# TensorE multiplies the identity into free banks, a fixed number of times, at nineteen places where it waits in norms, routers and at the end of the experts

## What is computed

```python
def layer_norm(x, g, b):
    mu = xf.mean(-1, keepdims=True)
    var = jnp.square(xf - mu).mean(-1, keepdims=True)
    y = (xf - mu) * lax.rsqrt(var + LN_EPS) * g + b
def moe(h, router_w, router_b, w_gate, w_up, w_down):
    aff = jax.nn.sigmoid((x @ router_w))
    sel_score = aff + router_b
    ...  # the best of 4 groups of experts, in it the best 2 of 4: chosen
    w = aff * chosen / sum
    for e in range(N_EXPERTS):                       # 16 experts, width 512
        he = (silu(x @ w_gate[e]) * (x @ w_up[e])) @ w_down[e]
        y = y + w[:, e:e + 1] * he
def first_block(...):
    for l in range(DEPTH):                           # 2 layers
        mix = retention(h, ...) if l < 1 else nsa_attention(h, ...)
        h = layer_norm(ALPHA * h + mix, ln_mix_g[l], ln_mix_b[l])
        h = layer_norm(ALPHA * h + moe(h, ...), ln_ffn_g[l], ln_ffn_b[l])
def second_block(...):
    mix = (gates[0] * y_ssd + gates[1] * y_att) @ w_out
    h = layer_norm_2(alpha * h + mix, ln1_g, ln1_b)
    f = jnp.square(relu(h @ w_up)) @ w_down
    h = layer_norm_2(alpha * h + f, ln2_g, ln2_b)
```

## Time and profile before

| | |
|---|---|
| median of 3 runs | 1574.66 us (1574.34 to 1576.18) |
| the profiled execution: its time | 1574.03 us |
| its span, first to last instruction | 1572.2 us |
| PE busy | 1426.0 us, 91% |
| DVE busy | 774.6 us, 49% |
| ACT busy | 557.0 us, 35% |
| mean granted clock of PE | 0.945 |

### The profile page before, as it was taken

How to read it: one execution, slowest core, us unless ns; L and a number is a source line. 1 busy time by engine, 2 the same in 40 slices (tenths; PEclk the granted TensorE clock), 3 DMA queues, 4 the chain that set the end, 5 groups by cost and what they waited for, 6 DMA issues and landing times. The chain is left out here.

```text
span 1572.2 us, 19843 instructions
## 1 busy us (share of the span) xinstructions
PE 1426.0 (91%) x8494; PEld 1066.1 (68%) x8494; DVE 774.6 (49%) x1040; ACT 557.0 (35%) x778; POOL 63.5 (4%) x73
## 2 busy tenths in 40 slices
PE   6999978999968989969999959999888899799996
PEld 6986764344326778854444339898867799699985
DVE  4646551222235647541221253599668865655545
ACT  3344321111012444321101023588447753335432
POOL 0000010000002000010000020000022100000000
PEclk9999978999997989969999969999898999999998
DMA  8544775999982520459999964423212135435451
GB/s 330 211 163 161 276 285 207 429 426 429 428 381 100 209 113 1 161 241 398 427 428 428 427 282 148 174 108 126 101 43 108 54 116 207 161 135 190 186 198 43
DMA packets 27600, 355.23 MB, mean 226 GB/s; under 512 B 2864, under 2 KB 4912, under 8 KB 5616
## 3 DMA queue, kind: packets, MB, share of 16 engines
q1 hardware_dynamic: 25696, 341.85, 54.4%
q0 software_dynamic: 1808, 12.01, 1.9%
HBM read 352.80 MB, written 1.05 MB: 225 GB/s over the span
## 5 line engine op out<-in xcount | busy, mean ns | idle before, releaser
L1931 DVE TENSOR_TENSOR ring_low<-ring,w_rounded 128x2048 fp32r<-128x2048 f32 (+1 forms) x128 | 291.3, 2276 | 318.6 <-ACT w_rounded L1479 310.7
L1479 ACT ACTIVATE w_rounded<-ring 128x2048 fp32r<-128x2048 f32 (+1 forms) x128 | 243.0, 1900 | 358.6 <-PE ps L826 128.3
L826 PE MATMUL ps<-split,w_rounded 128*128 128x256 f32 x1056 | 254.7, 291 | 22.7 <-DVE ring_low L1931 17.1
L826 PE MATMUL ps<-split,ring_low 128*128 128x256 f32 x800 | 231.4, 289 | 0.0
L826 PEld LDWEIGHTS ps<-split,w_rounded 128*128 128x128 f32 x1056 | 189.5, 197 | 25.1 <-issue 19.6
L842 PE MATMUL ps<-w_rounded,split 128*128 128x512 f32 (+1 forms) x448 | 157.0, 400 | 8.0 <-DVE ring_low L1931 3.4
L826 PE MATMUL ps<-hT_low,w_rounded 128*128 128x256 f32 x544 | 157.5, 289 | 0.0
L826 PEld LDWEIGHTS ps<-split,ring_low 128*128 128x128 f32 x800 | 157.4, 197 | 0.0
L842 PE MATMUL ps<-ring_low,split 128*128 128x512 f32 (+1 forms) x304 | 119.1, 392 | 0.0
L2171 DVE TENSOR_SCALAR split<-ps,work 128x1024 fp32r<-128x1024 f32 x14 | 18.0, 1284 | 197.6 <-PE ps L1014 197.6
L826 PEld LDWEIGHTS ps<-hT_low,w_rounded 128*128 128x128 f32 x544 | 108.3, 199 | 0.0
(11 more groups left out here) (333 smaller groups left out, 2206.9 us busy)
## 6 DMA issues: line engine op xcount, KB each, us to landing
ring<-slabs SPq DMA_DIRECT2D x65, 2048.0 KB, 7.8
work<-experts_w SPq DMA_DIRECT2D x48, 2048.0 KB, 20.3
ring<-experts_w SPq DMA_DIRECT2D x36, 2048.0 KB, 16.9
w_plain<-experts_w SPq DMA_DIRECT2D x12, 2048.0 KB, 16.7
gb<-ln_gb POOLq DMA_DIRECT2D x6, 1024.0 KB, 7.9
ring<-slabs SPq DMA_DIRECT2D x2, 1024.0 KB, 8.8
hT<-x_feat SPq DMA_DIRECT2D x1, 1024.0 KB, 5.1
work<-c_ret POOLq DMA_DIRECT2D x1, 1024.0 KB, 11.9
```

The costliest lines, as they stand in the source:

```text
L826: last = nc.tensor.matmul(dst[:, at:at + T], w3[a][:, k, c * P:(c + 1) * P], src[b][:, k, :], start=(k == 0 and t == 0), stop=(k == KC - 1 ...
L1479: nc.scalar.activation(rounded_half(q), half_of(ring, q), ACT.Copy).then_inc(w_high, 1)
L1931: V.tensor_tensor(half_of(ring_low, q), half_of(ring, q), rounded_half(q).bitcast(F32), ALU.subtract).then_inc(w_low, 1)
```

## The change

A helper `idle_products(dst, n)` issues n plain f32 products of the identity with the identity repeated twice (256 moving columns) into a PSUM bank which nothing reads before it is written anew. No semaphore is signalled by them. They stand ahead of waits: before each tile's transposes in norms 0 to 4 and after the last of them (table `IDLE`), before the position products (8), before the first gather (3), and before `scatter_tail` (13). That is 14 + 21 + 10 + 21 + 20 = 86 in the norms and 2 x (8 + 3 + 13) = 48 in the rest, 134 in all. Where n is 0 behind the transposes nothing is issued, but `take_aux` still adds its wait for the first transposed bank to be free, which `wait_transposed` waits for as well.

```diff
+            def idle_products(dst, n):
+
+                out2 = dst[:, 0:2 * P].rearrange("p (a n) -> p a n", a=2)
+                for _ in range(n):
+                    nc.tensor.matmul(out2, ident, ident.unsqueeze(1).broadcast_to([P, 2, P]), start=True, stop=True)
+
+            IDLE = {"ln0": (9, 5, 0), "ln1": (12, 5, 4), "ln2": (5, 5, 0), "ln3": (12, 5, 4), "ln4": (10, 4, 6)}
+
             def tokens_to_features(stage, src, groups, ready, first):
 
                 for i in range(NT):
+                    after_experts = i == 0 and stage in ("ln1", "ln3")
+                    idle_products(bank(0) if after_experts else take_aux(AX[stage] + groups * i), IDLE[stage][i])
                     pe.wait_ge(ready, first + i)
                     for c in range(groups):
                         transpose4(AX[stage] + groups * i + c,
...
             def norm_to_features(n):
                 tokens_to_features(f"ln{n}", h, 2, h_ready, 2 * n + 1)
+                idle_products(take_aux(AX[f"ln{n}"] + 4), IDLE[f"ln{n}"][2])
                 wait_transposed(f"ln{n}", 4)
...
                 if q is None:
+                    idle_products(bank(0), 13)
                     scatter_tail(e2)
...
                 pos = take_aux(AX[f"router{layer}"] + 1)
+                idle_products(pos, 8)
                 pe.wait_ge(member_ready, layer + 1)
...
                 pe.wait_ge(token_low, NT * layer + NT)
+                idle_products(bank(0), 3)
                 expert_pass(passes[layer][0])
```

## The result

The changed kernel's median is **1563.18 us** (1559.5 to 1566.05, 5 runs) against 1574.88 (1574.34 to 1576.18, 5 runs) before: ratio 0.9919, 95% interval 0.9899 to 0.9939. It is 11.7 us faster, where 17.7 were forecast. The profiled execution took 1561.76 us, 12.27 less than that of before.

The account below looks back on a forecast made before the run. The clock halved at norms and routers, so PE waited and then worked slowly. Products in the waits would give back 6.6 + 6.4 + 4.5 + 4.5 + 1.7 = 23.7 us, less 6.0 for routers: 17.7, to 1557 us, range 1550 to 1567.

Parts of the forecast that it names:

- Price of a product, 0.43: On PE, a product of two records takes 0.43 us at full clock, 0.86 at 1.2 GHz.
- What hides the products: At the norms, routers and experts' ends, each group at 0.43 us a product fits PE's wait; at 0.86 none fits.
- Norm 4, 1.7: After norm 4, 17 records of `up` would run at full clock, gaining 1.7 us; its second transposes nothing.
- Second transposes, 0.88: In four norms, the second eight transposes would take 1.09 us instead of 1.97, gaining 0.88 each.
- Routers, 6.6 and 6.4 less 3.0 each: Norms with routers 0 and 1 gain 6.6 and 6.4 us, less 3.0 each as the clock falls within the router.
- the row: At 228 to 230 PE was busy all 2.00 us with 16-column router records, yet the clock stayed at 0.50.
- Does the gain reach the end?: The gain was to reach the end: the experts' slab stream moves with PE, and later projections are PE's own chain.
- the case forecast: Whole kernel: products hold the clock but it falls within the routers; 1553 to 1563 us, chance 0.60.
- rival (c): Routers cost about what they give, the clock falling before them; 5 to 11 us gained, 1563 to 1569, chance 0.17.
- (d): Slower: products don't hold the clock, each takes 0.86 and overruns its wait; about 48 us, 1622, chance 0.06.
- (e): No change: the clock falls as before between groups, which stay hidden in their waits; chance 0.04.
- Rival (b): The clock holds through the routers too; the full 23.7 us gained, 1551 us, chance 0.13.

Follow-up runs that it names:

- e2: The changed kernel with as many products at the same places, each moving 16 columns instead of 256; 1576.59 us, ratio 1.0009 to before.
- e8: The changed kernel with 20 products instead of 9 ahead of norm 0's first transposes; 1564.17 us in a single execution.
- e1: The changed kernel with the twelve products of norms 1 and 3 ahead of the overflow branch instead of behind it; 1558.62 us, ratio 0.9901 to before.
- e6: e5 plus two products between the second transposes and the router in norms 0 and 2; 1550.70 us, ratio 0.9857 to before.
- e5: e1 with norm 4's last six products sent to bank 0, which is free all that time; 1560.47 us, ratio 0.9906 to before.
- e11: The changed kernel plus only the two products behind the second transposes of norms 0 and 2; 1559.35 us, ratio 0.9898 to before.
- e10: The kernel of e6 measured again, unchanged; 1549.78 us, ratio 0.9837 to before.
- e9: The kernel of e5 measured again, unchanged; 1560.08 us, ratio 0.9906 to before.
- e12: e6 with six products instead of eight ahead of the positions; 1557.13 us, ratio 0.9876 to before.
- e7: e5 with five products instead of eight ahead of the positions; 1554.49 us, ratio 0.9878 to before.
- e3: The changed kernel with only the 8 + 3 products of each router left; 1574.19 us, ratio 0.9988 to before.
- e4: The changed kernel with only the products of the norms left, none of the 13, 8 and 3; 1570.12 us, ratio 0.9967 to before.

## Why the prediction came out as it did

**What bounds the kernel, and that the gain is the clock.** Right. e2 has as many products with fewer columns, a clock that fell ahead of the router all the same, and no gain.

**Price of a product, 0.43.** Right: 0.216 a record in after, and e8.

**What hides the products.** Right for norms 0, 2 and the 13; wrong for the twelve at the end of the experts. The step that failed is "end of the experts, ... 12 in 5.2 of 5.98": it took the wait of the earlier trace rows as free for PE from its first microsecond. 3.3 to 4.8 us at the start of it were the branch, and nothing that stands behind it was issued meanwhile. The products started 2.98 and 4.12 us late, at a clock that had fallen, and the places gave 2.75 and 1.20 us instead of 4.5 each. That is 5.0 of the missing time. With the products ahead of the branch norm 1 gives 4.52 (e1), and norm 3 gives 4.41 in e6, where the stall that cut it to 2.85 in e1 is absent: the term itself was right.

**Norm 4, 1.7.** Sized right, but the text on the kernel held that `take_aux` adds only a wait that is there anyway. For products ahead of `wait_transposed` it is a new one, 1.71 us, and it made `up` 0.4 us late: 1.07. With a free bank 1.57 (e5).

**Second transposes, 0.88.** Right (1.97 to 1.09 in norm 0). They gained at a clock held by the products, and so against the sentence of the Trainium skill (TensorE: Matmul & The Clock Gate, Part 4) that the full clock doesn't engage for transposes.

**Routers, 6.6 and 6.4 less 3.0 each.** The full terms are right almost to the tenth: 32.12 - 25.50 = 6.62 in e11 and 29.80 - 23.16 = 6.64 in e6. The fall inside the router is right too. The loss was smaller than 3.0 in the profile of after: 2.5 and 0.6, because the router fell late (0.6 and 0.1 lost, not 1.6) and the gather did not suffer at all. One part was too low, positions 1.92 late in router 0 instead of 0.9: the rise took longer than the 3.3 us taken from the gather (the eight began at 231.92, and 235 to 238 still shows 0.59). The small loss is in part the luck of one execution: e5 and e11 lost 2.5 in router 1 as well (25.64 and 25.66). In after the clock fell within the router while PE was busy with it, and in e2 it stayed at 0.50 over 10.4 us of narrow products back to back. Both speak for the row, and against the rule of the Trainium skill (TensorE: Matmul & The Clock Gate, Part 1), time in sustained matmul activity, as the prediction applied it.

**Does the gain reach the end?** Right within the experts: 0.04 and 0.27 us were lost in some 217 each. But the last 65 us of sparse attention, untouched, took 3.06 us more. The stretch 640 to 650, in before and in after:

```profile
640.00:650.00 10.00, 10.00 (x66) 8.79 (x66) 5.86 (x16) 1.09 (x2) 0.00 (x0) 1.00 0.27 115
```

```profile
640.00:650.00 10.00, 10.00 (x34) 8.07 (x34) 1.83 (x6) 0.00 (x0) 0.00 (x0) 0.66 0.50 182
```

In after the clock is down for a part of it. Those 65 us last 65.1, 66.7 or 68.2 us in each of the fourteen profiles, and both ends occur with kernels that differ by nothing ahead of it (e6 65.11, e10, the same kernel, 68.17). So the change doesn't force the long one: the length differs between executions of one kernel, and the profile of before was one of the short ones. Whether the change makes the long ones more frequent was not counted. Executions of one kernel spread accordingly: over 6.6 us in the 5 runs of after, over 8.3 us in the 23 runs of before beside e1 (1571.81 to 1580.1).

**The number.** 17.7 forecast, 14.9 at the touched places, 12.3 in the profiled execution, 11.7 between the medians. By groups, the ends of the experts fell short by 5.05 (2.75 + 1.20 for 9.0), norm 4 by 0.63, and the routers were 2.88 better (4.10 + 5.78 for 7.0): 17.7 - 5.05 - 0.63 + 2.88 = 14.9. The routers' surplus hides about half of what the other groups lack, so the total looks better than the terms. The time, 1563.18, lies 0.2 above the case forecast (1553 to 1563), where the range of rival (c) begins; by its mechanism it is the case forecast. The reason of (c), routers that give nothing, did not occur (4.10 and 5.78). Rivals (d) and (e) are refuted by the clock row. Rival (b)'s time was reached by e6, 24 us gained. It isn't quite (b): its places give 21.2 us in the profile (router 0 still fell), and 2.7 came from untouched parts.

**What stays open.** Between the kernel of e5 and that of e6 lie 9.8 us in the medians, and 10.3 in the repeat. In the first pair of profiles router 1 accounts for 2.5 and the stall in norm 3's transposes for 1.8. In the second router 1 accounts for nothing and the stall for 1.6, and the two profiled executions took the same time (1556.78 us for e9, its fastest, 1556.46 for e10, its slowest). The stall (1.43 to 1.68 us on "issue", within the first eight transposes of norm 3) is in e1, e5, e9 and e12 and absent in e6, e7 and e10; the two kernels that were profiled twice show it both times or neither. The 57 us behind that norm, which no edit touches, took 57.2 us in each of the four with it and 55.6 to 56.4 in the three without. So some 3 us of the distance go with the stall, and the two kernels without it, those of e6 and e7, are the two fastest. Part of what looks like the worth of products added or taken away (e6, e7, e12) may be owed to it alone. No kernel has the stall changed by itself, so that stays unproven, and the rest of the 10 us is not located. The stall comes soon after the branch; that the supply of instructions is late there is an argument and was not tested.

## What to carry to other kernels

Idle time on an engine's row is not free for new work by itself: look at the sequencer's records of that stretch too, and put filler ahead of a branch, and into a buffer that needs no wait. Each group of filler must start at full clock and fit its wait, so a group can depend on the one before it (router 0: 0.8 and 0.7 us alone, 4.1 together). Where the clock falls differs between executions of one kernel, so one profile can't rank two placements. And since kernels that differ by a few products differed by 6 to 10 us in a way that no sum foretold, try a few neighbours on the chip and compare medians rather than single executions.

## What the runs showed of the hardware

- The compare-and-branch on PE's sequencer, which is not taken, lasts 3.30 to 5.30 us over all profiles (28 instances). Matmuls issued before it ran on meanwhile (5.34 us of them in e1); none behind it did (idle 2.98 and 4.12 us in after).
- PE stood without instructions for 1.43 to 1.68 us within eight equal transposes soon after that branch, in three of the five kernels with the products ahead of the branch (e1, e5, e12) and not in the other two (e6, e7); repeats of e5 and e6 agree.
- With products of 16 columns back to back for 10.4 us the clock stayed at 0.50 (e2), and it fell to 0.50 during 4.34 us of them in after; with groups of products of 256 columns it was 1.00 through a norm with idle times of 0.57 and 1.21 us. The full clock served transposes: 1.09 us for eight, against 1.97.
- The last 65 us of sparse attention, unchanged, took 65.1, 66.7 or 68.2 us in all fourteen profiles, by a fall of the clock inside them (0.66 in 640 to 650 in after, 1.00 in before), and two executions of one kernel took 65.1 and 68.2.
